# Value rows of product-key experts: from half on VectorE, half on TensorE, to all on TensorE in 64x64 quarters

## The chip, the cores and the metric

The kernel runs on one core of one Trainium2 chip. The metric is the device time of one execution in microseconds (us). All data are fp32.

## What is computed

Two decoder layers over 256 tokens of width 1024, each followed by a product-key expert layer (PEER) with a table of 16384 rows. Layer 0 mixes by sparse attention and retention, layer 1 by a convolution module. The change is in the expert layer, cut here to what matters:

```python
def peer_ffn(h, w_q, sub_keys, u, v):
    q = (xf @ w_q).reshape(T, P_HEADS, 2, P_QDIM // 2)
    s1, s2 = ...                       # two sets of 128 scores for each of 8 heads
    v1, i1 = lax.top_k(s1, 16); v2, i2 = lax.top_k(s2, 16)
    sv, ci = lax.top_k(all 256 sums of v1 and v2, 16)
    eidx = ...                         # 8 heads x 16 picks = 128 rows of the table for each token
    gate = softmax(sv)
    hb = einsum('td,tkd->tk', xb, u[ib])
    act = gelu(hb) * gb
    return einsum('tk,tkd->td', act, v[ib])
```

Each token thus takes 128 picks per layer. A pick is a row of `u` (1024 numbers, for the dot product) and a row of `v` (1024 numbers, for the weighted sum).

## The kernel before, in words

The tokens form two tiles of 128, one token per partition. There are four expert phases `p` = 0 to 3: layer 0 tile 0, layer 0 tile 1, layer 1 tile 0, layer 1 tile 1. A phase has 8 rounds of 16 picks, and a round 4 batches of 4 picks (`RING = 16`, `BATCH = 4`).

The table holds `u` and `v` side by side, 8 KB a row. POOL issues one indirect DMA per pick (`gathers`, L414) that brings one row for each of the 128 tokens, 1 MB, into one of 16 slots of `ring`. It runs at most five gathers ahead of the last one landed (`AHEAD = 5`), and before it fills a slot again it waits for both users of the slot: `v_added` (VectorE) and `v_multiplied` (TensorE). At the start of each round it waits for the slot 0 of the round before, and copies 16 indices (L397).

VectorE (`expert_round`) takes a dot product of each landed slot with the token row (L892, into `hb`). After each batch ScalarE applies Gelu (L562), multiplies with the gate (L566, `act_v`) and writes a 128x128 diagonal matrix with the four weights (L573, `diag`). The weighted sum is split by columns. The first 512 columns are added on VectorE, straight into the residual `x_tok` (L900), four picks behind the dot products. The other 512 are multiplied on TensorE, which accumulates `diag` times the slot in one PSUM bank, `acc` (L1284). `open_sum` puts the residual into `acc` by a product with the identity (L1277), and `close_sum` copies it back (L915):

```python
                pe.matmul(acc, ident[:, :], x_tok[:, p % 2, HALF:D], start=True, stop=False)
...
                    pe.matmul(acc, diag[:, r % (2 * BATCH), :], ring[:, r, D + HALF:2 * D],
                              start=False, stop=(last and r == RING - 1)) \
                        .then_inc(v_multiplied, 1)
...
                dve.tensor_copy(x_tok[:, p % 2, HALF:D], acc).then_inc(x_ready, 1)
```

The order on each engine is written out by hand, and other work is put between the rounds and batches. Beside the rounds of phase 0, and the last four of phases 1 and 2, the product-key heads of the next picks are computed: TensorE makes queries and scores between batches (`heads_in_steps`, L1042, L1263), with a weight chunk of 1 MB for each head, and VectorE picks the best after each round (`heads`). Such rounds are called heads rounds here. Beside the first four rounds of phases 1 and 2 runs the convolution module of the other tile (`conv_beside` on TensorE and ScalarE; `conv_pair` L943, `conv_centre`, `conv_norm`, `conv_out` on VectorE). The last phase has nothing beside it.

Weights come in chunks of 1 MB through SyncE's queue into two buffers (`load_chunks`); a chunk is asked for when the product that used its buffer is done. On the chip all transfers share the same DMA engines.

An fp32 product shows as two weight loads and two matmul records in the trace.

## Time and profile before

| what | value |
|---|---|
| median of 3 runs | 1746.88 us (1746.08 to 1751.19) |
| profiled execution, its span | 1750.9 us (it has no separate time; the span is taken for it) |
| VectorE busy | 1428.1 us, 82% |
| TensorE busy, matmul | 1002.7 us, 57% |
| TensorE weight loads busy | 610.9 us, 35% |
| ScalarE busy | 498.4 us, 28% |
| POOL busy | 775.9 us, 44% |
| moved by DMA | 625.78 MB, mean 357 GB/s |

The rows further down are of four kinds. A group of instructions has its count, its busy time, the mean of one in ns, and the idle time of the engine before it with what ended it. A window gives the busy time of each engine in a stretch, the granted TensorE clock (1.00 is 2.4 GHz, 0.50 is 1.2 GHz), the DMA share (mean busy share of the core's 16 DMA engines; over 1 when packets overlap) and the rate. A timeline merges neighbouring instructions of one kind: start, length, count. Busy shares of the whole span are means over stages that have different limits.

### The profile page before, as it was taken

The page shows a single profiled execution, that of the slowest core. Times are in us where ns is not written, and L with a number is a line of the kernel's source. Part 1 is how long each engine was busy: PE and PEld are TensorE (multiplying, and loading weights), DVE is VectorE, ACT ScalarE, POOL GpSimd, SP SyncE. Part 2 cuts the span into 40 slices and gives each one's busy share as a digit, 9 for nine tenths or more (in the row PEclk, how much of TensorE's full clock was granted, in tenths as well). Part 3 has the DMA queues.
Part 4 walks back from the last instruction along what each step waited for, and adds up shares of the span by engine and source line. Part 5 has one row for each costly group of instructions (what it writes and reads, how often), then busy time and mean ns, then how long its engine had stood idle before and what let it go on. Part 6 is the DMA issues. An engine that isn't in the chain of part 4 may idle for free.

```text
span 1750.9 us, 17116 instructions
## 1 busy us (share of the span) xinstructions
PE 1002.7 (57%) x3934; PEld 610.9 (35%) x3934; DVE 1428.1 (82%) x3330; ACT 498.4 (28%) x1442; POOL 775.9 (44%) x565
## 2 busy tenths in 40 slices
PE   7998663555443653465455555355644456555655
PEld 7785442333331331333333333133422332222222
DVE  2755594999999889894999999988599999877776
ACT  2222220333222522232223242223222233222222
POOL 0003431434434578852344448874333345544551
PEclk9999777787777886676777777678777777776777
DMA  9147989799999999898999998899899998999996
GB/s 356 55 133 301 410 303 366 290 379 385 385 384 402 420 364 368 315 393 318 408 389 378 402 371 338 323 341 418 310 382 395 406 394 335 422 422 422 422 422 266
DMA packets 149994, 625.78 MB, mean 357 GB/s; under 512 B 9648, under 2 KB 76976, under 8 KB 84400
## 3 DMA queue, kind: packets, MB, share of 16 engines
q0 software_dynamic: 73728, 536.90, 75.7%
q1 hardware_dynamic: 76208, 88.20, 14.8%
q8 instruction: 24, 0.39, 0.1%
q14 instruction: 34, 0.28, 0.0%
HBM read 624.02 MB, written 1.05 MB: 357 GB/s over the span
## 4 chain that ended last, share of the span: by engine, by line
DVE 43%; PE 20%; DMA 17%; issue 11%; ACT 4%; DVEq 3%; ACTq 1%; POOL 0%; POOLq 0%
DVE ring L892 15%; DMA ring<-experts_dram,idx_now 11%; DVE x_tok L900 9%; PE pm L1042 9%; PE side L1284 7%; DVE conv_buf L943 7%; DMA wbuf<-w_o_dram 3%; DMA wbuf<-w_dram 3%; ACT act_v L566 1%; PE side L1042 1%; DVE top_i L825 1%; DVE rest L826 1%; DVE top_i L838 1%; ACTq L569 1%; DVE best_i L844 1%
## 5 line engine op out<-in xcount | busy, mean ns | idle before, releaser
L414 POOL DMA_INDIRECT ring<-experts_dram,idx_now x512 | 745.4, 1456 | 633.5 <-DMA ring<-experts_dram,idx_now 247.1
L1284 PE MATMUL side<-ring,diag 128*128 128x512 f32 x1024 | 597.0, 737 | 555.7 <-ACT diag L573 555.6
L892 DVE SCALAR_TENSOR_TENSOR ring<-ring,h_tok 128x1024 f32<-128x1024 f32 x512 | 615.7, 1220 | 55.8 <-DMA ring<-experts_dram,idx_now 50.7
L1284 PEld LDWEIGHTS side<-ring,diag 128*128 128x128 f32 x1024 | 232.6, 239 | 863.9 <-ACT diag L573 625.4
L900 DVE SCALAR_TENSOR_TENSOR x_tok<-ring,act_v,x_tok 128x512 f32<-128x512 f32 x512 | 383.8, 750 | 26.1 <-ACT act_v L566 20.3
L562 ACT ACTIVATE ge<-hb 128x4 f32<-128x4 f32 x128 | 26.3, 205 | 701.3 <-DVE ring L892 701.3
L573 ACT ACTIVATE diag<-ident,act_v 128x128 f32<-128x128 f32 x512 | 163.8, 390 | 15.9 <-issue 2.2
L397 POOL COPY idx_now<-eidx 128x16 uint32 x32 | 24.3, 760 | 258.1 <-DVE x_tok L900 184.3
L943 DVE SCALAR_TENSOR_TENSOR conv_buf<-conv_buf,chan_sb 128x128 f32<-128x128 f32 x480 | 126.7, 347 | 0.0
L1042 PEld LDWEIGHTS side<-h_t,wbuf 128*128 128x128 f32 x1024 | 119.3, 192 | 15.3 <-issue 15.3
L1042 PE MATMUL side<-h_t,wbuf 128*128 128x128 f32 x1024 | 119.5, 275 | 0.0
L566 ACT ACTIVATE act_v<-ge,gates 128x1 f32<-128x1 f32 x512 | 109.0, 283 | 15.6 <-issue 10.9
L1042 PE MATMUL pm<-h_t,wbuf 128*128 128x128 f32 x512 | 63.8, 286 | 21.8 <-DMA wbuf<-w_dram 21.8
L1042 PEld LDWEIGHTS pm<-h_t,wbuf 128*128 128x128 f32 x512 | 63.4, 202 | 30.4 <-DMA wbuf<-w_dram 23.5
L553 ACT ACTIVATE expo<-lead 128x16 f32<-128x16 f32 x32 | 6.6, 208 | 227.6 <-DVE lead L853 227.6
L822 DVE MAX8 top_v<-side 128x8 f32<-128x128 f32 x64 | 15.6, 288 | 63.7 <-PE side L1263 63.7
L562 ACT ACT_TABLE_LOAD x46 | 59.0, 1283 | 3.4 <-issue 2.5
L1042 PE MATMUL pm<-conv_buf,ring 128*128 128x128 f32 x448 | 53.7, 280 | 0.2 <-DVE ring L770 0.2
L1042 PEld LDWEIGHTS pm<-conv_buf,ring 128*128 128x128 f32 x448 | 52.3, 194 | 1.4 <-DVE ring L770 0.6
L1042 PE MATMUL pm<-wbuf,h_t 128*128 128x256 f32 x128 | 33.4, 420 | 27.2 <-DMA wbuf<-w_dram 23.1
L1042 PE MATMUL pm<-wbuf,conv_buf 128*128 128x256 f32 x64 | 22.9, 536 | 42.2 <-DMA wbuf<-w_o_dram 42.2
L1036 PE MATMUL pm<-ident,h_tok 128*128 128x128 f32 x56 | 12.6, 405 | 57.5 <-DVE h_tok L663 57.5
(188 smaller groups left out, 838.0 us busy)
## 6 DMA issues: line engine op xcount, KB each, us to landing
wbuf<-wq_dram SPq DMA_DIRECT2D x32, 1024.0 KB, 25.8
wbuf<-w_dram SPq DMA_DIRECT2D x24, 1024.0 KB, 19.8
ring<-w_in_dram SPq DMA_DIRECT2D x5, 2048.0 KB, 20.0
wbuf<-w_o_dram SPq DMA_DIRECT2D x8, 1024.0 KB, 17.1
ring<-experts_dram,idx_now POOLq DMA_INDIRECT x512, 11.5
gain<-gains_dram SPq DMA_DIRECT2D x7, 512.0 KB, 13.9
ring<-w_in_dram SPq DMA_DIRECT2D x1, 1696.0 KB, 10.1
x_tok<-x_dram SPq DMA_DIRECT2D x2, 512.0 KB, 4.7
```

Of the source, the lines that this page charges most:

```text
L397: pool.tensor_copy(idx_now[:, half, :], eidx[:, t, ds(i * (2 * RING) + half * RING, RING)]) \
L414: pool.indirect_dma_start(ring[:, r, :], None, table[layer], bass.IndirectOffsetOnAxis(idx_now[:, half, r:r + 1], 0)) \
L562: act.activation(ge[:, c], hb[:, c], ACT.Gelu)
L566: last = act.activation(act_v[:, r:r + 1], ge[:, r:r + 1], ACT.Copy, scale=gates[:, t, ds(i * RING + r, 1)])
L569: act.drain()
L573: act.activation(diag[:, (b % 2) * BATCH + j, :], ident[:, :], ACT.Copy, scale=act_v[:, r:r + 1]).then_inc(diag_ready, 1)
L825: dve.max_index(top_i[:, b, j, 0:8], top_v[:, b, j, 0:8], side[b, j])
L892: dve.scalar_tensor_tensor(out=ring[:, r, 0:D], in0=ring[:, r, 0:D], scalar=1.0, in1=h_tok[:, t, :], op0=ALU.mult, op1=ALU.mult, accum_out ...
L900: dve.scalar_tensor_tensor(out=xs, in0=ring[:, r, D:D + HALF], scalar=act_v[:, r:r + 1], in1=xs, op0=ALU.mult, op1=ALU.add).then_inc(v_add ...
L943: step = dve.scalar_tensor_tensor(out=dst, in0=src, scalar=tap, in1=dst, op0=ALU.mult, op1=ALU.add)
L1042: last = pe.matmul(dst, lhs(k), rhs(k), start=(k == 0), stop=(k == KD - 1))
L1284: pe.matmul(acc, diag[:, r % (2 * BATCH), :], ring[:, r, D + HALF:2 * D], start=False, stop=(last and r == RING - 1)) \
```

## The change

The weighted sum moves wholly to TensorE. Two picks are taken together, and each of their products is cut into quarters: 64 rows (tokens) by 64 columns of the array. For tokens 0 to 63, the even pick goes to PSUM partitions 0 to 63 and the odd one to 64 to 127; for tokens 64 to 127 the reverse. With two row halves, two halves of the 1024 columns (`c`) and two picks a pair has eight products of 64x64 by 512. The sums stand in four PSUM banks, `acc[half][c]`, and each bank holds two partial sums, of even and of odd picks, which `close_sum` adds across partitions. The diagonals are 64 wide. The candidates of the heads (`cand`) leave PSUM for SBUF, and the products of the convolution and of the attention output share two banks of `pm` where they had four.

```diff
-HALF = D // 2
+HALF = P // 2
+COLS = D // 2
...
-        diag = sb("diag", [P, 2 * BATCH, P])
+        diag_all = sb("diag_all", [P, 8 * P])
+        diag = diag_all[:, 0:2 * BATCH * HALF].rearrange("p (k c) -> p k c", k=2 * BATCH)
+        cand = diag_all[:, 4 * P:8 * P].rearrange("p (h a b) -> p h a b", h=2, a=P_TOP)
+        ident2 = sb("ident2", [P, HALF])
...
-        acc = side[:, 2, :]
-        cand = side[:, 3, :].rearrange("p (h a b) -> p h a b", h=2, a=P_TOP)
+        acc = [[side[:, 2, :], side[:, 3, :]], [pm[:, 1024:1536], pm[:, 1536:2048]]]
...
-                            pool.wait_ge(v_added, i * (2 * RING) + freed)
                             pool.wait_ge(v_multiplied, i * (2 * RING) + freed)
...
-                        act.activation(diag[:, (b % 2) * BATCH + j, :], ident[:, :], ACT.Copy,
+                        act.activation(diag[:, (b % 2) * BATCH + j, :], ident2[:, :], ACT.Copy,
                                        scale=act_v[:, r:r + 1]).then_inc(diag_ready, 1)
...
-                def add_v(r):
-                    n = p * PICKS + r
-                    if r % BATCH == 0:
-                        dve.wait_ge(act_ready, i * RING + (n + BATCH))
-                    dve.wait_ge(v_added, i * RING + (n + RING))
-                    dve.scalar_tensor_tensor(out=xs, in0=ring[:, r, D:D + HALF], scalar=act_v[:, r:r + 1], in1=xs,
-                                             op0=ALU.mult, op1=ALU.add).then_inc(v_added, 1)
...
             def close_sum(p):
 
+                t = p % 2
                 dve.wait_ge(v_multiplied, RING + (p + 1) * PICKS)
-                dve.tensor_copy(x_tok[:, p % 2, HALF:D], acc).then_inc(x_ready, 1)
+                for i in range(2):
+                    rows = slice(i * HALF, (i + 1) * HALF)
+                    for c in range(2):
+                        dve.tensor_copy(x_tok[rows, t, c * COLS:(c + 1) * COLS], acc[i][c][rows, :])
+                dve.drain()
+                for i in range(2):
+                    rows, others = slice(i * HALF, (i + 1) * HALF), slice((1 - i) * HALF, (2 - i) * HALF)
+                    for c in range(2):
+                        xs = x_tok[rows, t, c * COLS:(c + 1) * COLS]
+                        last = dve.tensor_tensor(xs, xs, acc[i][c][others, :], ALU.add)
+                last.then_inc(x_ready, 1)
...
-                for r in range(RING):
-                    n = p * PICKS + r
-                    pe.wait_ge(diag_ready, i * RING + (n + 1))
-                    pe.matmul(acc, diag[:, r % (2 * BATCH), :], ring[:, r, D + HALF:2 * D],
-                              start=False, stop=(last and r == RING - 1)) \
-                        .then_inc(v_multiplied, 1)
...
+                for r0 in range(0, RING, 2):
+                    n = p * PICKS + r0
+                    pe.wait_ge(diag_ready, i * RING + (n + 2))
+                    pe.sem_inc(pair_on, 1)
+                    for c in range(2):
+                        for r in (r0, r0 + 1):
+                            for half in range(2):
+                                rows = slice(half * HALF, (half + 1) * HALF)
+                                j = (half + r) % 2
+                                step = pe.matmul(acc[half][c][j * HALF:(j + 1) * HALF, :], diag[rows, r % (2 * BATCH), :],
+                                                 ring[rows, r, D + c * COLS:D + (c + 1) * COLS],
+                                                 start=False, stop=(last and r >= RING - 2))
+                            if c:
+                                step.then_inc(v_multiplied, 1)
```

Two more edits follow from the banks. `open_sum` has eight quarter products for one. The first two additions of the attention output of tile 1 (`add_projected`) stand one round earlier, and TensorE waits for them before it uses their bank again; in the convolution, a product waits for the glu of the tile two before it, not four.

On TensorE, the first batches of phase 0. Before, four full products stood between two queries (in these rows `side` and `pm` are PSUM, `diag` the diagonals, `ring` the slots, `wbuf` a weight chunk):

```order
L1284 MATMUL side<-ring,diag 128x512 x4
L1042 MATMUL side<-h_t,wbuf 128x128 x16
L1284 MATMUL side<-ring,diag 128x512 x4
L1042 MATMUL side<-h_t,wbuf 128x128 x16
L1284 MATMUL side<-ring,diag 128x512 x4
L1263 MATMUL side<-keys_sb,q_t 128x128 x2
```

Now the last pair of picks of the third batch, up to the scores, reads:

```order
L1298 MATMUL side<-ring,diag_all 64x512
L1298 MATMUL pm<-ring,diag_all 64x512
L1298 MATMUL side<-ring,diag_all 64x512
L1298 MATMUL pm<-ring,diag_all 64x512
L1298 MATMUL side<-ring,diag_all 64x512
L1298 MATMUL pm<-ring,diag_all 64x512
L1298 MATMUL side<-ring,diag_all 64x512
L1298 MATMUL pm<-ring,diag_all 64x512
L1265 MATMUL side<-keys_sb,q_t 128x128 x2
L1042 MATMUL pm<-wbuf,conv_buf 128x256 x8
```

Each row of four products with 128x512 (one batch) has become two pairs of eight with 64x512, alternating between the banks of the two token halves.

On VectorE, the end of phase 0 before:

```order
L892 SCALAR_TENSOR_TENSOR ring,hb<-ring,h_tok 128x1024
L900 SCALAR_TENSOR_TENSOR x_tok<-ring,act_v,x_tok 128x512
L892 SCALAR_TENSOR_TENSOR ring,hb<-ring,h_tok 128x1024
L900 SCALAR_TENSOR_TENSOR x_tok<-ring,act_v,x_tok 128x512 x5
L915 COPY x_tok<-side 128x512
L659 RECIPROCAL rstd<-root 128x1
L663 SCALAR_TENSOR_TENSOR h_tok<-x_tok,rstd,gain 128x1024
L924 MEMSET conv_buf 128x8x30
L892 SCALAR_TENSOR_TENSOR ring,hb<-ring,h_tok 128x1024 x5
```

And now:

```order
L897 SCALAR_TENSOR_TENSOR ring,hb<-ring,h_tok 128x1024 x16
L907 COPY x_tok<-side 64x512 x2
L907 COPY x_tok<-pm 64x512 x2
L913 TENSOR_TENSOR x_tok<-x_tok,side 64x512 x2
L913 TENSOR_TENSOR x_tok<-x_tok,pm 64x512 x2
L664 RECIPROCAL rstd<-root 128x1
L668 SCALAR_TENSOR_TENSOR h_tok<-x_tok,rstd,gain 128x1024
L923 MEMSET conv_buf 128x8x30
```

The 16 dot products of the round stand in one row with nothing between them, and closing the sum is eight instructions of 64 partitions.

On POOL, from the tenth slot of a round to the start of the next, with the semaphores waited for. Before:

```order
L414 DMA ring<-experts_dram,idx_now 128x2048 [waits gathered9,v_added,v_multiplied]
L414 DMA ring<-experts_dram,idx_now 128x2048 [waits gathered10,v_added,v_multiplied]
L394 REGISTER_ALU
L395 REGISTER_ALU [waits picks_ready]
L397 ISA [waits v_added]
L397 COPY idx_now<-eidx 128x16
L414 DMA ring<-experts_dram,idx_now 128x2048 [waits gathered11,v_multiplied,idx_copied,v_added]
```

And now:

```order
L418 DMA ring<-experts_dram,idx_now 128x2048 [waits v_multiplied,gathered9]
L418 DMA ring<-experts_dram,idx_now 128x2048 [waits v_multiplied,gathered10]
L399 REGISTER_ALU
L400 REGISTER_ALU [waits picks_ready]
L402 ISA [waits v_multiplied]
L402 COPY idx_now<-eidx 128x16
L418 DMA ring<-experts_dram,idx_now 128x2048 [waits gathered11,idx_copied,v_multiplied]
```

The waits for VectorE's additions are gone, and the copy of the next indices, too, waits for TensorE.

## Rows read from the trace of the kernel before

**Rows 1.** The page, 40 equal slices of the span: busy tenths, DMA tenths, GB/s

```profile
DVE  2755594999999889894999999988599999877776
...
DMA  9147989799999999898999998899899998999996
GB/s 356 55 133 301 410 303 366 290 379 385 385 384 402 420 364 368 315 393 318 408 389 378 402 371 338 323 341 418 310 382 395 406 394 335 422 422 422 422 422 266
```

**Rows 2.** Windows: us, busy PE, PEld, DVE, ACT, POOL, TensorE clock, DMA share, GB/s

```profile
405.00:453.60 48.60, 25.22 (x104) 15.36 (x104) 44.76 (x116) 13.16 (x44) 19.51 (x17) 0.75 0.98 388
...
587.10:819.50 232.40, 126.75 (x488) 79.71 (x488) 195.62 (x468) 73.51 (x181) 148.28 (x71) 0.75 0.93 364
...
1015.40:1246.80 231.40, 124.91 (x488) 79.72 (x487) 195.74 (x468) 73.49 (x181) 146.73 (x68) 0.77 0.90 352
...
1503.10:1701.70 198.60, 112.77 (x158) 43.08 (x157) 152.31 (x242) 53.11 (x185) 98.48 (x85) 0.75 1.01 422
```

**Rows 3.** Windows: full traffic, a dip, and the two stretches of the sum

```profile
374.00:412.00 38.00, 13.29 (x60) 8.41 (x59) 34.10 (x99) 10.11 (x34) 12.18 (x13) 0.76 1.02 411
...
803.00:809.00 6.00, 6.00 (x19) 4.39 (x18) 0.42 (x1) 0.00 (x0) 0.00 (x0) 0.70 0.39 128
...
318.00:1472.70 1154.70, 614.49 (x2416) 375.11 (x2415) 1029.61 (x2534) 348.03 (x1014) 580.21 (x383) 0.76 0.95 373
1472.70:1735.70 263.00, 155.51 (x219) 59.23 (x217) 207.36 (x330) 70.73 (x249) 128.69 (x108) 0.75 1.00 418
```

**Rows 4.** Timeline of VectorE in a heads round: start us, us

```profile
406.15 1.22 DVE L892 SCALAR_TENSOR_TENSOR ring<-ring,h_tok 128x1024 f32<-128x1024 f32 x1
...
407.30 1.22 DVE L892 SCALAR_TENSOR_TENSOR ring<-ring,h_tok 128x1024 f32<-128x1024 f32 x1
...
427.88 1.22 DVE L892 SCALAR_TENSOR_TENSOR ring<-ring,h_tok 128x1024 f32<-128x1024 f32 x1
...
429.69 1.23 DVE L892 SCALAR_TENSOR_TENSOR ring<-ring,h_tok 128x1024 f32<-128x1024 f32 x1
```

**Rows 5.** The page, groups by line, and a DMA issue with its us to landing

```profile
L414 POOL DMA_INDIRECT ring<-experts_dram,idx_now x512 | 745.4, 1456 | 633.5 <-DMA ring<-experts_dram,idx_now 247.1
L1284 PE MATMUL side<-ring,diag 128*128 128x512 f32 x1024 | 597.0, 737 | 555.7 <-ACT diag L573 555.6
...
L900 DVE SCALAR_TENSOR_TENSOR x_tok<-ring,act_v,x_tok 128x512 f32<-128x512 f32 x512 | 383.8, 750 | 26.1 <-ACT act_v L566 20.3
...
L943 DVE SCALAR_TENSOR_TENSOR conv_buf<-conv_buf,chan_sb 128x128 f32<-128x128 f32 x480 | 126.7, 347 | 0.0
...
L915 DVE COPY x_tok<-side 128x512 f32<-128x512 f32 x4 | 2.8, 692 | 6.0 <-PE side L1284 6.0
...
ring<-experts_dram,idx_now POOLq DMA_INDIRECT x512, 11.5
```

**Rows 6.** Timeline of TensorE (last row: chain of waits): start us, us, records

```profile
42.60 1.15 PE L1105 MATMUL side<-ring 32*128 32x256 f32 x16
...
89.08 1.09 PE L1193 MATMUL side<-ring 128*64 128x128 f32 x16
...
102.25 7.07 PE L1042 MATMUL side<-wbuf,conv_buf 128*128 128x256 f32 x32
...
248.51 3.73 PE L1042 MATMUL side<-h_t,wbuf 128*128 128x128 f32 x32
...
432.77 3.70 PE side L1284 x8
```

**Rows 7.** Waits in 307 to 550 us: total us, times, longest

```profile
POOL idx_now L397 <- DVE x_tok L900: 57.3, 5, 22.0
...
POOL ring L414 <- PE side L1284: 25.1, 18, 2.0
```

**Rows 8.** The chain of waits, 754 to 822 us: start us, us

```profile
777.36 24.32 DMA wbuf<-w_dram
```

**Rows 9.** The page, an instruction queue: packets, MB, share

```profile
q8 instruction: 24, 0.39, 0.1%
```

More of the change, by code:

```diff
@@ L258, in hybrid_decoder_trunk_kernel @@
         a_at = [side_flat[:, 1536:2048], pm[:, 1536:2048]]
-        wo_at = [[side_flat[:, c * 512:c * 512 + WCOLS] for c in range(4)], [pm[:, c * 512:c * 512 + WCOLS] for c in range(4)]]
+        wo_at = [[side_flat[:, c * 512:c * 512 + WCOLS] for c in range(4)], [pm[:, c % 2 * 512:c % 2 * 512 + WCOLS] for c in range(4)]]
         def norm_at(e):
@@ L887, in expert_round @@
                 rounds = PICKS // RING
-                xs = x_tok[:, t, 0:HALF]
-                def dot(r):
+                for r in range(RING):
+                    if between:
+                        between(r)
                     dve.wait_ge(gathered[r], i * 16 + 16 * (p * rounds + 1))
@@ L991, in _ @@
             heads(0, 1)
+            for c in range(2):
+                add_projected(1, c)
             expert_round(0, 1)
             heads(0, 2)
-            for c in range(4):
+            for c in range(2, 4):
                 add_projected(1, c)
@@ L1204, in output_product @@
                 pe.wait_ge(b_t_ready, t + 1)
+                if t and c >= 2:
+                    pe.wait_ge(projected_added, 4 + c - 1)
                 w = chunk(W_O[t] + c + (t and c // 2 * 2))
@@ L1276, in open_sum @@
                     pe.wait_ge(x_ready, (0, 3, 5, 7)[p])
-                pe.matmul(acc, ident[:, :], x_tok[:, p % 2, HALF:D], start=True, stop=False)
-            def expert_round(p, i, between=None, last=False):
-                for r in range(RING):
-                    n = p * PICKS + r
-                    pe.wait_ge(diag_ready, i * RING + (n + 1))
-                    pe.matmul(acc, diag[:, r % (2 * BATCH), :], ring[:, r, D + HALF:2 * D],
-                              start=False, stop=(last and r == RING - 1)) \
-                        .then_inc(v_multiplied, 1)
-                    if between and (r + 1) % BATCH == 0:
-                        between(r // BATCH)
+                for c in range(2):
+                    for j in range(2):
+                        for i in range(2):
+                            rows = slice(i * HALF, (i + 1) * HALF)
+                            out_rows = slice(j * HALF, (j + 1) * HALF)
+                            pe.matmul(acc[i][c][out_rows, :], ident[rows, out_rows], x_tok[rows, p % 2, c * COLS:(c + 1) * COLS],
+                                      start=True, stop=False)
+            def expert_round(p, i, between=None, last=False):
+                for r0 in range(0, RING, 2):
+                    n = p * PICKS + r0
+                    pe.wait_ge(diag_ready, i * RING + (n + 2))
+                    pe.sem_inc(pair_on, 1)
+                    for c in range(2):
+                        for r in (r0, r0 + 1):
[7 more added lines that the diff above has]
+                                step.then_inc(v_multiplied, 1)
+                    if between and (r0 + 2) % BATCH == 0:
+                        between(r0 // BATCH)
             def conv_in(t, c):
@@ L1294, in conv_in @@
                 for j in range(2):
-                    last = product(pm[:, (c % 4) * 512 + j * P:(c % 4) * 512 + (j + 1) * P],
+                    last = product(pm[:, c % 2 * 512 + j * P:c % 2 * 512 + (j + 1) * P],
                                    lambda k: w[:, k, j * P:(j + 1) * P], lambda k: h_t[:, k, :])
```

36 lines of the change are left out of this document (15 added, 21 removed).

## The prediction, made before the changed kernel ran

> **What bounds the kernel now.** I read the page's slices first [rows 1]. VectorE is mostly at 8 or 9 tenths from the eighth slice to the thirty-fourth, and that invites the conclusion that VectorE is the bound. The transfer rows beneath say more: the DMA engines are at 8 or 9 tenths in the same slices, and the rate only settles at 422 GB/s in the last stage.
>
> So the stages have to be read one by one. By the windows [rows 2], the last stage (1503 to 1702 us, five of the eight rounds of the last token tile) has DMA share 1.01 and 422 GB/s: it is bound by transfers, and nothing VectorE does less can shorten it. A round with product-key heads (405.0 to 453.6 us, 48.6 us for 16 picks and two weight chunks of 1 MB) has VectorE busy 44.8 us, yet the DMA share is already 0.98 at 388 GB/s. The convolution stages (587.1 to 819.5 and 1015.4 to 1246.8 us) have 0.93 and 0.90 at 364 and 352 GB/s. Where the transfers lose time is seen by cutting finer [rows 3]: undisturbed traffic of picks with weights beside it (374 to 412 us) runs at share 1.02 and 411 GB/s, while a dip such as 803 to 809 us has 0.39. The waits of POOL, which issues the gathers, name the cause [rows 7]: in 307 to 550 us it stood 57.3 us before the copy of the next 16 indices, waiting for a ring slot that VectorE's addition frees. The kernel is thus bound by transfers that VectorE interrupts. VectorE's time is worth only the gaps that it tears into them.
>
> **The change part by part.** *Taken from VectorE:* 512 additions at L900, 750 ns of one and 383.8 us together [rows 5]. Start to start, two dot products without an addition between them are 1.15 us apart and with one 1.81 us [rows 4]; 16 dot products then take 18.4 us instead of 29. A heads round on VectorE falls from 48.6 to about 18.4 + 22.7 = 41.1 us, where 22.7 us is what lies between the end of dot product 16 (430.9 us) and the next first one (453.6 us). That is below what its transfers need, so they become the bound.
>
> *Put on TensorE:* the other 512 columns. Each pick had one 128x512 product, two matmul records; warm, eight records take 3.70 us [rows 6], so 0.93 us per pick with start-up and 0.86 without. Now a pair of picks has eight 64-row, 64-column products over 512 columns. If the four quarters run together, two groups of two records each take 4 x 0.43 = 1.7 us per pair, 0.86 per pick: no more than now. Whether they do decides the case. The trace shows both halves of it. Two column halves (L1193, 128*64) do 16 records of 128 columns in 1.09 us, though 32 records on the full array take 3.73 us, 0.117 each. Four row groups (L1105, 32*128) do 16 records of 256 columns in 1.15 us, where the full array takes 7.07 us for 32, 0.22 each [rows 6]. So rows together and columns together each overlap nearly ideally; both at once appears nowhere. I take 0.86 us warm (about 1.7 at the half clock), and between there and four times that lie the rivals.
>
> The Trainium skill, "TensorE: Matmul & The Clock Gate", Part 3, gives measured gains of packing below the ideal, 3.07 times for four row tiles and 6.32 for nine in both directions; by 3.07 an estimate for a pick would be 1.1 us warm, which would still lie under the transfers and leave the sum as it is. The trace agrees for rows alone: 16 x 0.22 = 3.5 us against 1.15 is 3.1 times.
>
> *ScalarE:* the diagonals halve in width. I cost that at nothing: the chain of Gelu, gate and four diagonals remains. *POOL:* each gather waits on one semaphore less, but slots come back in pairs and only from TensorE, so slot 0 is free, and the index copy can start, up to one pair later (3.4 us at the half clock). The granted clock averages 0.75 there [rows 2], a mix of the two levels. Nearly hidden: five gathers are in flight, at 2.5 us each (198.6 us / 80 in the last stage) or 2.9 beside weights (45.9 / 16, below).
>
> *Closing a tile's sum:* one copy of 0.69 us [rows 5] becomes four copies, a drain and four additions over 64 partitions and the same 512 columns. The number of partitions has no row; by the columns it is 8 x 0.69 = 5.5 us, 4.8 more, between half of it (if 64 partitions were cheaper) and 6 with the drain. Four times: the last is on the path to the output and counts in full; the other three lie in breaks in which gathers go on. Opening a sum is 8 products for one, under 1 us more, hidden by the Gelu chain of the first batch. The candidates move from PSUM to SBUF, the convolution's products share two banks instead of four and are reused after two; the glu they wait for comes from a step that VectorE has by then passed, so nothing. Two additions of the attention output move one round earlier, 0.4 us each, nothing.
>
> *The sum.* Up to 318 us: no change. VectorE waits there for products behind weight chunks, which the edit leaves. From 318 to 1472.7 us, 1154.7 us at share 0.95 and 373 GB/s [rows 3]. Filled without gaps, by the share it would be 1154.7 x 0.95 / 1.02 = 1075 us, by the bytes 1154.7 x 373 / 411 = 1048 us: a gain of 80 or 107, and I take the middle, 93, since the weights' small packets cost share that the bytes don't show. Not all gaps close. Two convolution stages still end behind a weight chunk that takes 24.3 us to land [rows 8] while TensorE, and with it four ring slots, stands; two tiles close with about 29 us before the next dot product (5.6 waiting for the last products, from 430.9 to 436.5 us in the heads round, 5.5 closing, 17 heads, which is the rest of the 22.7, and one norm of about a dot product), against eleven gathers of 2.5 to 2.9 us that can still be issued. I leave 5 us for each of these four and 5 for the twelve heads rounds: 25 us. Gain 93 - 25 = 68. From 1472.7 to 1735.7 us: share 1.00, gain 0. Tail: 4.8 us more. Together 63 us less: the profiled execution's 1750.9 us become 1688, and the median of the runs, 1746.9 us, which lies 4 us below it, becomes **1684 us**.
>
> **The rivals.** *A, the forecast:* four quarters together, transfers filled. Own range 1645 (all 107, no gap left) to 1717 us (80, with the gaps taken at 45). Chance 0.60.
>
> *B, latency keeps the gaps:* the dips in the convolution stages and tile breaks are made by the wait for weight chunks and by long VectorE blocks that remain. Then only the twelve heads rounds gain, from 48.6 to 45.9 us (48.6 x 388 / 411), 32 us, less 4.8: 27 us, 1720 us. For it: the 24.3 us wait. Against: the dips also follow the blocks of 15.8 us of convolution (126.7 us / 8) [rows 5], during which the ring would now be less behind. Chance 0.18.
>
> *C, only two quarters at once:* 1.71 us per pick warm. A heads round has 16 x 1.71 + 8 us of other products, 35 of 46 us, so TensorE isn't the bound, but every slot comes back later and I would leave 60 us of gaps instead of 25: 1719 us. Chance 0.08.
>
> *D, one quarter at a time:* this ends slower. 3.43 us per pick, 55 + 8 = 63 us for a heads round against 48.6 (13 rounds, with the one before 356 us; 187 us), 55 against 39.8 in the last tile (8 rounds, 121 us), and 39 more in each convolution stage (126.7 us busy now, 64 x 2.26 us more, against 232): about 2130 us. It decides from 2.4 us per pick on, (46 - 8) / 16. Against it are both overlaps in [rows 6]. Chance 0.08.
>
> *E, TensorE's loop is fetched anew in each pass:* a heads loop grows from 16 + 36 to 64 + 36 products, each four instructions, 208 to 400. One instruction queue moved 24 packets of together 0.39 MB [rows 9], 16 KB each, so the loop now spans more of them. If each pass had to fetch behind the gathers, with their 11.5 us to landing as the upper bound (the lower is nothing), slot 0 would come 11.5 us late in ten loop rounds: with 12 us idle in each, 1684 + 120 = 1804 us. Chance 0.06. The Trainium skill, "Runtime: NRT & Kernel Launch", Instruction fetch mechanics, says that a taken branch out of the present window forces such a fetch, and also that TensorE's instruction memory holds 2048 instructions, by which 400 would fit; no row here shows its size.
>
> **How the numbers follow.** The time is A's. A measurement of this kernel can tell 0.3% (5 us) from no change. A gives 0.58 faster and the rest to same and slower, B and C 0.20 faster, 0.05 same and 0.01 slower, D and E 0.14 slower: faster 0.78, same 0.06, slower 0.16. The range leaves out D and E and reaches over B and C: 1650 to 1730 us.
>
> **What would show it.** Right: quarter products starting some ns apart in fours, under 2 us per pair warm; dot products 1.15 us apart after each block; heads rounds of 45 to 47 us with share 1.01 or 1.02; convolution stages of 205 to 215 us; the last tile's rounds unchanged at 39.8 us; about 5 us more after the last product. Wrong: a pair of 3.4 us or more at the full clock (C, D), pauses of TensorE at each loop start (E), heads rounds faster but convolution stages still near 230 us (B), or heads rounds still at 48 us though VectorE stands idle in them.

## The result, and the profile of the changed kernel

The changed kernel takes 1771.25 us (median of 4 runs, 1766.83 to 1773.54); the kernel before, on the same chip, takes 1749.04 us (4 runs, 1746.08 to 1752.86). The ratio is 1.0116, with a 95% interval of 1.0092 to 1.0140: the change makes the kernel slower by 1.2%, where 3.6% faster was forecast. The profiled execution has a span of 1771.2 us against 1750.9 us.

The page first. Rows answer to [rows 1] and [rows 5]:

```profile
PE 1029.6 (58%) x7062; PEld 570.4 (32%) x7062; DVE 1098.6 (62%) x2846; ACT 468.2 (26%) x1442; POOL 746.3 (42%) x566
...
DVE  2655274666668877734766687691477766544454
...
GB/s 354 52 131 313 413 262 376 327 374 381 386 401 396 414 335 349 371 413 266 388 405 390 395 295 355 357 368 412 263 388 385 386 370 339 421 422 422 422 422 216
...
L1298 PE MATMUL side<-ring,diag_all 64*64 64x512 f32 x2048 | 585.6, 721 | 496.6 <-ACT diag_all L577 496.5
...
L826 DVE MAX8 top_v<-side 128x8 f32<-128x128 f32 x64 | 15.7, 290 | 211.3 <-PE side L1265 211.2
L974 DVE TENSOR_TENSOR x_tok<-x_tok,pm 128x256 f32<-128x256 f32 x8 | 3.0, 418 | 84.6 <-PE pm L1042 84.5
```

VectorE was relieved just as the diff says: it is busy in 62% of the span, and the slices that stood at 8 or 9 tenths stand mostly at 6 to 8. TensorE's products cost nothing extra (585.6 us where they had 597.0 [rows 5]; those into `pm`, 585.5 us, run beside those into `side`). Yet the mean rate of the transfers is 353 GB/s where it was 357, and the two slices just behind the convolution stages have fallen to 266 and 263 GB/s, from 318 and 310 [rows 1]. The last two rows of groups show where VectorE's freed time went: it is waited away, 211.2 us at the first operation of the heads and 84.5 us at the residual addition of the convolution.

The same in windows. Columns as in [rows 2]: us, busy PE, PEld, DVE, ACT, POOL, TensorE clock, DMA share, GB/s. In order: a heads round, the first and the second convolution stage, a round of the last tile, and 803 to 809 us.

```profile
403.30:451.90 48.60, 25.27 (x200) 13.46 (x200) 33.71 (x100) 12.10 (x44) 18.87 (x17) 0.75 0.97 384
...
582.20:819.80 237.60, 127.33 (x872) 76.22 (x872) 152.88 (x405) 70.04 (x181) 147.15 (x74) 0.77 0.95 376
...
1021.50:1254.00 232.50, 132.84 (x872) 78.14 (x871) 152.06 (x404) 70.10 (x181) 138.57 (x68) 0.76 0.91 356
...
1593.30:1633.10 39.80, 23.60 (x128) 7.56 (x128) 19.75 (x33) 9.76 (x37) 20.51 (x17) 0.71 1.01 422
...
803.00:809.00 6.00, 0.56 (x2) 0.50 (x2) 0.00 (x0) 0.00 (x0) 0.18 (x1) 0.50 1.02 411
```

A heads round lasts 48.60 us, to the tenth what it lasted before [rows 2], with 11 us less of VectorE in it. The first convolution stage is 5.2 us longer, with 43 us less of VectorE in it. And the dip at 803 to 809 us (0.39, 128 GB/s in [rows 3]) is gone: the transfers now run straight through it, and the stage is longer all the same. Measured from the first dot product of each round to the next, the whole adds up:

| stretch (us) | before | after | difference |
|---|---|---|---|
| start to round 3 | 356.3 | 353.7 | -2.6 |
| four heads rounds | 194.3 | 194.2 | -0.1 |
| last round of that tile (no heads) | 36.5 | 34.3 | -2.2 |
| first convolution stage | 232.4 | 237.6 | +5.2 |
| next four heads rounds (the one that closes a tile: 50.3, 55.4) | 195.9 | 201.7 | +5.8 |
| second convolution stage | 231.4 | 232.5 | +1.1 |
| next four heads rounds (the closing one: 50.1, 54.7) | 195.6 | 200.4 | +4.8 |
| last tile, to its last dot product | 294.6 | 296.6 | +2.0 |
| after the last dot product | 13.9 | 20.2 | +6.3 |

Inside the convolution stages the relief did pay at first: their first three rounds together take 156.9 and 154.1 us where they took 167.7 and 166.4. Their last rounds took it back, 80.6 and 78.4 us where they had 64.7 and 65.0.

So there are two questions: why twelve rounds of heads gained nothing, and what makes 20 us at the end of the convolution stages and where tiles close. The chain of waits answers the first, over one heads round (start us, us, what):

```profile
403.27 4.68 DVE ring L897 x8
...
410.07 1.08 PE side L1298
...
415.74 3.77 PE side L1042 x32
...
423.10 3.77 PE side L1042 x32
...
430.46 0.64 PE side L1265 x4
...
434.70 0.66 PE side L1265 x4
...
451.94 1.23 DVE ring L897
```

Four dot products (4.7 us), then Gelu and diagonals (2.1 us), and from 410.07 to 435.4 us TensorE without a pause: four batches of products (L1298), two queries of 3.77 us (L1042), and the scores of the two heads (L1265), the second of which stands in its queue **behind the last batch**. Only then can VectorE finish the heads, in 16.5 us, and start the next round. 4.7 + 2.1 + 25.3 + 16.5 = 48.6 us: this ring goes through TensorE, and it is as long as the whole round was before. In windows (columns as above), TensorE's piece and its first batch alone:

```profile
410.07:435.40 25.33, 25.27 (x200) 13.44 (x200) 12.12 (x24) 8.53 (x32) 11.54 (x11) 0.92 0.92 358
...
410.07:415.74 5.67, 5.67 (x33) 1.80 (x33) 5.67 (x11) 2.46 (x11) 0.91 (x2) 0.64 0.87 355
```

TensorE is busy in 25.27 of the 25.33 us. Behind 23.4 us of idleness its first batch is granted a mean clock of 0.64 and takes 5.7 us, where the later batches, at 1.00, take 3.6; that, too, is part of the ring.

The kernel before had the same ring already. In its round of 405.0 to 453.6 us TensorE worked from 411.52 to 436.9 us with one pause, of 0.17 us, before its last batch of products, and VectorE then stood 1.25 us for the scores behind that batch:

```profile
432.77 3.70 PE L1284 MATMUL side<-ring,diag 128*128 128x512 f32 x8 [0.17 <-ACT diag L573]
...
437.07 0.50 DVE L822 MAX8 top_v<-side 128x8 f32<-128x128 f32 x2 [1.25 <-PE side L1263]
```

In the changed kernel VectorE's timeline shows the wait (the last number in brackets is idle us before the operation, and what ended it):

```profile
421.61 0.08 DVE L897 DVE_READ_ACCUMULATOR ring<-ring,h_tok 128x1 f32 x1
431.25 0.50 DVE L826 MAX8 top_v<-side 128x8 f32<-128x128 f32 x2 [9.56 <-PE side L1265]
435.49 0.50 DVE L826 MAX8 top_v<-side 128x8 f32<-128x128 f32 x2 [3.74 <-PE side L1265]
```

For the first convolution stage, the chain of waits at its end, to be set beside the 24.32 us of [rows 8], and the transfers from 755 to 815 us by queue (packets, MB, share):

```profile
767.44 3.67 PE pm L1042 x16
...
771.12 37.18 DMA wbuf<-w_dram
...
808.44 6.21 PE pm L1042 x16
```

```profile
q0 software_dynamic: 2981, 21.68, 87.4%
q1 hardware_dynamic: 2883, 2.92, 14.5%
```

The fourth and last chunk of the second convolution weight needs 37.18 us to land. Between 755 and 815 us the gathers' queue (q0) moves 2981 packets and the weights' queue (q1) 2883, almost one for one; but a packet of a gather is a row of 8 KB, and one of a weight chunk a row of 1 KB, so weights get 49 of 410 GB/s. At that rate 1 MB takes 21 us by itself. The rest of the 37 us is the third chunk, asked for at 760.8 us and landed at about 787.3 us (TensorE starts on it at 787.4), with the fourth, asked for at 771.1 us, behind it.

The 24.32 us of [rows 8] belong to the third chunk, and it was not spared the crowd: while it was on its way in the kernel before, the two queues moved

```profile
q0 software_dynamic: 1189, 8.68, 86.7%
q1 hardware_dynamic: 1272, 1.29, 15.6%
```

again one for one. What differed was the fourth chunk. It was asked for at 790.7 us, and at 790.55 us POOL had issued its last gather for a while, since TensorE freed no slot:

```profile
809.50 0.93 POOL L414 DMA_INDIRECT ring<-experts_dram,idx_now  x1 [17.82 <-PE side L1284]
```

Once the gathers in flight had landed, the weights had the wires almost to themselves (794 of their packets against 55 from 802 to 808 us), and the fourth chunk landed in 16.9 us. The dip at 803 to 809 us was thus what let it through. From the request for the third chunk to the end of the stage it is 42.1 us before and 59.0 us after; the third chunk is asked for 11.7 us earlier in the stage now, and 16.9 - 11.7 makes the 5.2 us. The Trainium skill, "DMA: Bandwidth & Descriptors", Queues, rings and completion order, has each DMA engine go round its queues packet by packet; the trace agrees, with one packet for one as the profile counts them (2981 against 2883, and 1189 against 1272).

### The profile page after: what moved, and what is told of

Same layout as the page of the kernel before. It is cut to its first block, busy times and chain, and to the rows that moved or that the text cites. A ratio compares the mean times of both kernels' runs of the same rounds, so it can differ in the third digit from the quotient of the medians.

```text
span 1771.2 us, 22155 instructions
## 1 busy us (share of the span) xinstructions
PE 1029.6 (58%) x7062; PEld 570.4 (32%) x7062; DVE 1098.6 (62%) x2846; ACT 468.2 (26%) x1442; POOL 746.3 (42%) x566
## 4 chain that ended last, share of the span: by engine, by line
PE 36%; DMA 29%; DVE 25%; ACT 3%; issue 3%; DVEq 3%; ACTq 1%; POOL 0%; POOLq 0%
DMA ring<-experts_dram,idx_now 21%; PE side L1298 17%; PE pm L1042 9%; DVE ring L897 8%; PE side L1042 7%; DVE conv_buf L942 5%; DMA wbuf<-w_dram 4%; DMA wbuf<-w_o_dram 4%; PE side L1265 1%; DVE top_i L829 1%; ACT diag_all L577 1%; DVE rest L830 1%; ACT act_v L570 1%; DVE top_i L842 1%; PE pm L1298 1%
## 5 line engine op out<-in xcount | busy, mean ns | idle before, releaser
L418 POOL DMA_INDIRECT ring<-experts_dram,idx_now x512 | 718.5, 1403 | 635.1 <-issue 375.3
L1298 PE MATMUL side<-ring,diag_all 64*64 64x512 f32 x2048 | 585.6, 721 | 496.6 <-ACT diag_all L577 496.5
L897 DVE SCALAR_TENSOR_TENSOR ring<-ring,h_tok 128x1024 f32<-128x1024 f32 x512 | 599.8, 1224 | 171.0 <-DMA ring<-experts_dram,idx_now 165.8
L1298 PE MATMUL pm<-ring,diag_all 64*64 64x512 f32 x2048 | 585.5, 721 | 0.0
L1298 PEld LDWEIGHTS side<-ring,diag_all 64*64 64x64 f32 x2048 | 180.2, 162 | 835.5 <-issue 828.7
L1298 PEld LDWEIGHTS pm<-ring,diag_all 64*64 64x64 f32 x2048 | 165.8, 161 | 0.0
L826 DVE MAX8 top_v<-side 128x8 f32<-128x128 f32 x64 | 15.7, 290 | 211.3 <-PE side L1265 211.2
L577 ACT ACTIVATE diag_all<-ident,act_v 128x64 f32<-128x64 f32 x512 | 136.3, 336 | 17.3 <-issue 4.1
L1042 PEld LDWEIGHTS side<-h_t,wbuf 128*128 128x128 f32 x1024 | 116.8, 192 | 25.7 <-issue 25.7
L1042 PE MATMUL side<-h_t,wbuf 128*128 128x128 f32 x1024 | 122.6, 278 | 0.0
L1042 PE MATMUL pm<-h_t,wbuf 128*128 128x128 f32 x512 | 69.4, 300 | 26.5 <-DMA wbuf<-w_dram 26.5
L1042 PEld LDWEIGHTS pm<-h_t,wbuf 128*128 128x128 f32 x512 | 66.4, 213 | 40.4 <-DMA wbuf<-w_dram 30.0
L1042 PE MATMUL pm<-wbuf,h_t 128*128 128x256 f32 x128 | 38.8, 470 | 54.6 <-DMA wbuf<-w_dram 53.1
L974 DVE TENSOR_TENSOR x_tok<-x_tok,pm 128x256 f32<-128x256 f32 x8 | 3.0, 418 | 84.6 <-PE pm L1042 84.5
L1042 PE MATMUL pm<-conv_buf,ring 128*128 128x128 f32 x448 | 53.7, 280 | 0.2 <-DVE ring L774 0.2
L1042 PEld LDWEIGHTS pm<-conv_buf,ring 128*128 128x128 f32 x448 | 52.3, 194 | 1.4 <-DVE ring L774 0.6
## 6 DMA issues: line engine op xcount, KB each, us to landing
wbuf<-w_o_dram SPq DMA_DIRECT2D x8, 1024.0 KB, 21.7
ring<-experts_dram,idx_now POOLq DMA_INDIRECT x512, 11.7
```

Source lines behind the costliest of these rows:

```text
L418: pool.indirect_dma_start(ring[:, r, :], None, table[layer], bass.IndirectOffsetOnAxis(idx_now[:, half, r:r + 1], 0)) \
L577: act.activation(diag[:, (b % 2) * BATCH + j, :], ident2[:, :], ACT.Copy, scale=act_v[:, r:r + 1]).then_inc(diag_ready, 1)
L897: dve.scalar_tensor_tensor(out=ring[:, r, 0:D], in0=ring[:, r, 0:D], scalar=1.0, in1=h_tok[:, t, :], op0=ALU.mult, op1=ALU.mult, accum_out ...
L1042: last = pe.matmul(dst, lhs(k), rhs(k), start=(k == 0), stop=(k == KD - 1))
L1298: step = pe.matmul(acc[half][c][j * HALF:(j + 1) * HALF, :], diag[rows, r % (2 * BATCH), :], ring[rows, r, D + c * COLS:D + (c + 1) * COLS ...
```

## The experiments

The theory after this reading, **theory 1**: the heads rounds are held by the ring through TensorE, whose length is set by the scores standing behind the last batch, and the convolution stages by weight chunks that share the wires packet by packet. Its rivals: what holds the round is the amount of work on TensorE whatever its order, or the slots of the ring that come back in pairs, or the transfers of the round themselves.

**The scores ahead of the last batch.** TensorE's order in a heads round, alone (in all heads rounds but the first two of the kernel; indentation cut):

```diff
- between(r0 // BATCH)
+ b = r0 // BATCH
+ if not early or b < 2:
      between(b)
+ elif b == 2:
+     between(2)
+     between(3)
```

> Changed kernel, but TensorE makes the second head's scores before the last batch of picks and not after it. Theory 1 (a ring of waits: first batch of dot products, Gelu and diagonals, TensorE's whole round with both heads' products, then VectorE's heads, closes at 48.3 us): the heads can start 3.4 to 4.4 us sooner, heads rounds fall from 48.3 to 44.5 to 46 us, twelve of them give 30 to 45 us, median near 1733. Theory 2 (the transfers of a heads round, at share 0.97, are themselves the limit): rounds stay within 0.7 us of 48.3, median 1765 to 1771.

Measured: 1733.02 us (6 runs, 1721.53 to 1738.75), ratio 0.9901 to the kernel before (0.9865 to 0.9937). The heads rounds take 44.0 to 44.7 us; one of them in a window, and VectorE's timeline in it:

```profile
395.00:439.40 44.40, 24.56 (x200) 13.26 (x200) 33.81 (x101) 12.10 (x44) 19.99 (x17) 0.77 1.02 413
```

```profile
422.46 0.94 DVE L826 MAX8 top_v<-side 128x8 f32<-128x128 f32 x4 [7.76 <-PE side L1265]
```

Both heads' scores are there at 422.5 us, one wait instead of two, and the round runs at share 1.02 and 413 GB/s, the traffic that the prediction had asked for. The same instructions, on the same engines, in another order, are 38 us faster. The convolution stages' ends (rounds of 86.8 and 77.8 us) and the closings (55.3 and 54.7 us) do not get better, as theory 1 has it. Of VectorE's work, of the slots in pairs and of the amount of work on TensorE nothing was touched, and the round is 4.2 us shorter. That puts the transfers and the bare amount of work out as the bound of the 48.6 us; what the pairs cost by themselves no run shows.

**The same order in the kernel before.** The edit above, in the old loop.

> The kernel before with the same edit alone. There the four last additions (3.1 us) already cover most of the wait for the last batch, so theory 1 expects the heads 1.5 to 2.5 us sooner, heads rounds of about 46.5 us instead of 48.6, 18 to 30 us in all (median 1720 to 1732). Theory 2: nothing, 1747 to 1750.

Measured: 1737.13 us, ratio 0.9930 (0.9908 to 0.9953). The heads rounds fall from 48.6 to 47.3 us. The direction is right and the size too large: 1.3 us per round, and a median 5 us above the range. VectorE's own ring, with its additions, is just behind the one through TensorE: its last addition of the round ended at 435.4 us in the kernel before, 1.5 us ahead of the last scores. This is what two rings of nearly equal length mean in numbers: the reorder alone brings 1.3 us, the change alone nothing, both together 4.2 us.

**Half of the products.** The loop over the two column halves takes only the first; half of the weighted sum is left out, so this is not a version but a measure of TensorE's share.

```diff
-                     for c in range(2):
+                     for c in range(1):
...
-                             if c:
-                                 step.then_inc(v_multiplied, 1)
+                             step.then_inc(v_multiplied, 1)
```

> Changed kernel; the products of the second half of the 1024 columns are left out, so that half of the weighted sum is missing. TensorE's part of a round shrinks by 16 x 0.43 = 6.9 us and more at the half clock. Theory 1: heads rounds become bound by transfers, 45 to 46.5 us instead of 48.3, and slots come back sooner; median 1720 to 1740. Theory 2: heads rounds stay at 48, only the tail and the convolution rounds gain, median 1755 to 1770.

Measured: 1709.87 us (2 runs), ratio 0.9779 (0.9730 to 0.9828), 10 us below the range expected. Two heads rounds in one window:

```profile
382.90:473.20 90.30, 38.47 (x272) 23.68 (x272) 68.06 (x200) 24.30 (x88) 38.97 (x34) 0.73 1.02 412
```

45 us for a round at share 1.02 (single ones take 42 to 49 us): less work in the ring through TensorE lets the transfers fill, as less waiting does. The scores stand where they stood. So it is the length of the ring that counts, of which the place of the scores is one cause and the products another. Fewer products also give the slots back sooner, so this run alone does not speak against the rival of the slots; the reorder, which leaves them in pairs, shows that the pairs do not keep the round at 48.6 us.

**Closing without the additions.** The drain and the four additions of the closing are removed; one half of each pair's sum is left out.

```diff
-                 dve.drain()
-                 for i in range(2):
...
-                         last = dve.tensor_tensor(xs, xs, acc[i][c][others, :], ALU.add)
```

> Changed kernel; closing a sum only copies, so that of every two picks one is missing from the result. Closing falls from 5.2 to 2.6 us, four times. If all four closings lie on the path: 10 us less, median 1761. If only the last does: 2.6 us, 1769.

Measured: 1765.46 us (4 runs, 1760.59 to 1767.14), ratio 1.0100 (1.0064 to 1.0136). That is 6 us below the changed kernel by the medians, between the two expectations, but the intervals of the two ratios overlap, so the total alone does not show a gain. The traces do: the closing rounds take 52.6 and 52.4 us instead of 55.4 and 54.7, and the part after the last dot product 16.4 us instead of 20.2, of which 2.6 us are the additions and 1.2 a shorter wait for the last products. At the first of the four closings nothing is seen (the two rounds around it take 75.7 and 75.6 us).

**The second convolution weight in long rows.** Only this weight is laid out by chunks in HBM, so that a chunk of 1 MB is 128 rows of 8 KB instead of 1024 of 1 KB.

```diff
-                     sp.dma_start(wbuf[:, n % WBUF, :, :], view[:, :, c * WCOLS:(c + 1) * WCOLS]) \
+                     if len(view.shape) == 2:
+                         dst, src = wbuf[:, n % WBUF, :, :].rearrange("p k c -> p (k c)"), view[c * P:(c + 1) * P, :]
...
+                     sp.dma_start(dst, src) \
...
+def by_chunk(w):
+
+    return w.reshape(KD, P, -1, WCOLS).transpose(2, 1, 0, 3).reshape(-1, KD * WCOLS)
```

> Changed kernel; only the convolution's second weight matrix is laid out so that a 1 MB chunk is 128 rows of 8 KB, as a gather is, where it was 1024 rows of 1 KB. Theory 3 (the chunk lands late because the DMA engines share by packet, 360 GB/s of gathers against 50 of weights): these chunks land in 5 to 10 us instead of 25 and 35, the last round of each convolution stage falls from 80.6 and 78.4 us to 52 to 62, median 1731 to 1750. Theory 4 (the block at the end of the stage is made by TensorE's order and VectorE's steps): landing times change, but the rounds by less than 8 us each, median above 1758.

Measured: 1745.68 us (10 runs, 1738.98 to 1756.48, the slowest being the profiled one), ratio 0.9966 (0.9949 to 0.9984). The chain of waits over the same place:

```profile
780.73 9.04 DMA wbuf<-w_dram
...
795.25 37.72 DMA wbuf<-wq_dram
```

The chunk that took 37.18 us takes 9.04, and the stages' last rounds fall from 80.6 and 78.4 to 53.0 and 53.2 us. But the rounds behind them grow from 48.6 and 48.3 to 63.8 and 65.5 us. A chunk of query weights, still in rows of 1 KB, now stands in the chain there with 37.72 us, but it can't be all that makes these rounds long, as the next experiment shows. Of the 52.8 us by which the last rounds got shorter, 32.4 came back in the rounds behind them.

**All weights in long rows**, in the changed kernel, and **the same in the kernel before**:

> Changed kernel with all 64 weight chunks in rows of 8 KB. Theory 3: also the first two rounds (70 and 66 us, behind chunks of the output projection) fall to about 50 us each, the heads rounds stay near 48 us because they are bound by TensorE's round and the heads behind it; median 1685 to 1710.

> The kernel before with all weight chunks in rows of 8 KB. Heads rounds stay at 48.6 us (VectorE), the first two fall from 70 to 50 to 55 us, the convolution stages lose the waits for chunks but stay bound by VectorE at 210 to 220 us; median 1685 to 1705. The change would then still be worth nothing by itself.

Measured: 1705.59 us (4 runs, ratio 0.9744, 0.9709 to 0.9779) and 1693.50 us (4 runs, ratio 0.9682, 0.9652 to 0.9712). With short weight rows the change costs 22 us, with long ones 12. So some 10 of its 22 us are the late chunks. The rounds behind the convolution stages stay long in the changed kernel, 63 and 59 us, with no short row left. The first of them in a window:

```profile
754.10:817.40 63.30, 31.36 (x208) 16.57 (x208) 34.57 (x102) 14.48 (x46) 24.62 (x23) 0.72 1.01 421
```

The transfers fill it without a gap: 22 gathers land in it, six more than a round uses, since the stage before it ended with its gathers still to come. So the last round of a stage and the round behind it must be read together: the first such pair takes 129.3 us in the changed kernel and 113.2 us with long rows, 113.3 us in the kernel before and 103.9 us with long rows. The other heads rounds stay at 48.0 to 49.5 us in the changed kernel and at 48.3 to 48.8 in the one before, and the closings stay (54.9 and 54.2 against 50.2 and 50.0). The closings and the tail cover the 12 us: they are 4.7, 4.2 and 5.0 us longer than in the kernel before with long rows.

The convolution stages of the kernel before were 232.4 and 231.4 us [rows 2]. With long rows they are, a little above the 210 to 220 us expected:

```profile
549.30:771.70 222.40, 123.53 (x488) 77.52 (x488) 195.70 (x469) 73.52 (x181) 143.93 (x71) 0.76 0.91 374
967.50:1186.90 219.40, 121.15 (x488) 76.36 (x487) 195.60 (x467) 73.50 (x181) 144.78 (x68) 0.78 0.89 360
```

**Both edits together**, in the changed kernel, and in the kernel before:

> Changed kernel with early scores and all weights in rows of 8 KB: both causes taken away. Heads rounds near 44 to 45 us (18 transfers of 1 MB at 422 GB/s are 44.7 us), first rounds 50 us, convolution stages 200 to 210 us: median 1640 to 1665, below both kernels.

> The kernel before (half of the sum on VectorE) with early scores and all weights in rows of 8 KB: the same two edits as in the fastest run, without the change. Theory 1 has VectorE as the bound of a heads round here, 47.3 us as with early scores alone, so the median is 1675 to 1685, and the change is worth 12 to 22 us once the two other limits are gone. Rival (the change is worth nothing even then, all the gain is the two edits): 1658 to 1668.

Measured: 1662.69 us (4 runs, 1653.84 to 1671.06), ratio 0.9502 (0.9450 to 0.9553), and 1684.11 us (3 runs, 1678.66 to 1691.56), ratio 0.9601 (0.9565 to 0.9637). Each median is within its expected range. Windows of the changed kernel with both edits, a heads round and the two convolution stages:

```profile
365.80:410.80 45.00, 25.18 (x200) 13.38 (x200) 33.68 (x101) 12.10 (x44) 19.73 (x17) 0.77 1.01 418
535.50:749.30 213.80, 127.75 (x872) 71.89 (x872) 152.73 (x405) 70.04 (x181) 142.58 (x69) 0.78 0.91 373
944.30:1148.10 203.80, 123.32 (x872) 70.42 (x871) 151.95 (x403) 70.11 (x181) 136.37 (x63) 0.79 0.90 364
```

The change itself is worth 1684.1 - 1662.7 = 21 us by the medians and 1.0% (17 us) by the ratios, once what it waits for is out of the way. These two kernels ran on different chips, each beside the kernel before; the intervals do not overlap. By the traces most of it lies in the convolution stages, which take 224.2 and 222.5 us in the kernel before with both edits. The very same move of additions to TensorE costs 22 us in one surrounding and gains about 20 in another.

**The heads ahead of the closing.** In the fastest version so far, the last half of the heads goes ahead of the closing of the tile on VectorE.

```diff
                  expert_round(p, 7)
-                 close_sum(p)
                  heads(p + 1, 3)
+                 close_sum(p)
```

> Changed kernel with early scores and long rows, and VectorE computes the last heads of phases 1 and 2 before it closes the sum, so that the wait for the last products (6.7 us) lies under the heads. The rounds that close a tile fall from 55.8 and 54.7 to about 51 us if VectorE's block is what counts; 3 to 8 us in all, median 1655 to 1660. If the transfers refill the loss anyway: no difference from 1663.

Measured: 1657.77 us (4 runs, 1653.32 to 1661.27), ratio 0.9461 (0.9429 to 0.9492). The closing rounds fall by 1.3 and 1.0 us only, to 54.5 and 53.7 us, not to the 51 us expected. Its chain of waits shows why:

```profile
937.55 1.29 DVE x_tok L917 x2
...
938.86 1.06 ACT h_tok L439
...
940.06 1.28 ACT L441
...
941.36 0.30 ACT root L441
```

The eight instructions of the closing no longer wait for the last products, but ScalarE's part of the norm (square, table load and root, 1.06 + 1.28 + 0.30 us), which before lay beneath the heads, now stands open behind them. One exposed stretch was exchanged for another. It is the fastest version measured and beats both kernels of the case, by 92 us the one before; whether it beats the previous one can't be told (5 us, overlapping intervals).

## Why the prediction was wrong, point by point

**The bound.** "The kernel is thus bound by transfers that VectorE interrupts." The first half holds for the last tile (39.8 us a round before and after), and the second was only one of two causes. The wait that the prediction read from [rows 7], POOL for VectorE's addition, is real, 57.3 us; what it hid is that a ring of the same length through TensorE stood directly behind it, with only 0.17 us of pause in it. Over the whole run of the changed kernel the waits (total us, times, longest) read:

```profile
POOL idx_now L402 <- PE pm L1298: 226.6, 17, 27.7
DVE top_v L826 <- PE side L1265: 211.2, 28, 23.3
...
DVE x_tok L974 <- PE pm L1042: 84.5, 3, 41.9
```

Before, the first was 184.3 us (19 times, for VectorE), the second and the third 63.7 us (15 times) and 41.6 us (4 times, 14.4 at most). POOL stands before the same copy of indices as in [rows 7], with the releaser changed from VectorE to TensorE.

**The step that failed: "A heads round on VectorE falls from 48.6 to about 18.4 + 22.7 = 41.1 us ... That is below what its transfers need, so they become the bound."** The 18.4 us was right (the dot products are 1.15 us apart, the last one ends at 421.6 us). The 22.7 us was not a constant. It is 5.6 us of waiting for the last products and 17 us of heads, as the prediction itself splits it. The 17 us held (16.5). The 5.6 us were counted from the last dot product, as if the products came at a fixed distance behind it; but it is the end of TensorE's piece that sets them, and that hangs on the first batch of the round and not on the last dot product. The last scores leave TensorE at 435.4 us whatever VectorE does; with the last dot product done at 421.7 us the wait became 13.7 us, the block after the dot products 30.2 us (421.7 to 451.9), and 18.4 + 30.2 = 48.6. The prediction had TensorE's busy time (25.2 us of 48.6 [rows 2]) and compared only such totals with the round ("35 of 46 us, so TensorE isn't the bound", in rival C). Half idle was right; but its 25 us lie in one piece, in the middle of a ring whose other parts, 4.7 + 2.1 + 16.5 us, cannot lie beside them. The reorder and the halved products show it from two sides. The prediction's own last sign, "heads rounds still at 48 us though VectorE stands idle in them", is what came.

**The gaps of the convolution stages** (5 us for each taken off the gain). The prediction named the chunk of 24.3 us and took the wait as a constant too. Of the pair of chunks at a stage's end it is the other one that changed: 16.9 us before, in part with no gather beside it, and 37.2 us with the gathers flowing. The gap that the prediction counted as lost traffic was the time in which that chunk got through. Rival B had the stages stay near 230 us; they became 237.6 and 232.5, so even B was too friendly here. The runs with long rows show that the landing of chunks is worth 10 us of the change's loss, and 56 us to the kernel before on its own. Of those 56, some 36 are in the first two rounds (69.2 and 70.2 us, now 50.8 and 52.2), which the prediction left alone, and 21 at the ends of the two stages.

**The closings** (4.8 us, "the last ... counts in full; the other three lie in breaks in which gathers go on"). The price per closing was about right: 5.2 us for the eight instructions, 1.3 per pair, where the sum had 5.5. Timeline of VectorE at the end:

```profile
1759.80 1.28 DVE L907 COPY x_tok<-side 64x512 f32<-64x512 f32 x2 [8.75 <-PE pm L1298]
1761.09 1.30 DVE L907 COPY x_tok<-pm 64x512 f32<-64x512 f32 x2
1762.47 1.30 DVE L913 TENSOR_TENSOR x_tok<-x_tok,side 64x512 f32<-64x512 f32 x2
1763.78 1.28 DVE L913 TENSOR_TENSOR x_tok<-x_tok,pm 64x512 f32<-64x512 f32 x2
```

The tail grew by 6.3 us, 4.6 from this and most of the rest from the last batch of products (6.6 us where it had 5.2). Two of the other three closings are on the path as well, 4.6 to 5.1 us each; the removal of the additions took 2.8 and 2.3 us from them. With the heads rounds bound by a ring, a longer block on VectorE has no gathers to hide under.

**What was right.** The four quarters run at once (rival C and D are out), as the timeline of TensorE in the last tile shows:

```profile
1604.08 0.61 PE L1298 MATMUL side<-ring,diag_all 64*64 64x512 f32 x1 [4.09 <-ACT diag_all L577]
1604.09 0.64 PE L1298 MATMUL pm<-ring,diag_all 64*64 64x512 f32 x1
1604.10 0.64 PE L1298 MATMUL side<-ring,diag_all 64*64 64x512 f32 x1
1604.10 0.64 PE L1298 MATMUL pm<-ring,diag_all 64*64 64x512 f32 x1
1604.53 0.59 PE L1298 MATMUL side<-ring,diag_all 64*64 64x512 f32 x1
```

Four records start within 0.02 us, the next four 0.45 us after the first: four such steps are 1.7 us for a pair, as reckoned from the row halves and column halves of [rows 6]. Rival E is out: the instruction queue that moved 24 packets moves 38 in the whole run, and none from the second to the fourth pass of the first heads loop (403.3 to 547.9 us), though each pass should have fetched. The rounds of the last tile stayed at 39.8 us from the third on. The transfers' price of a heads round without gaps, 45.9 us in rival B, was reached (44.4 us), but only by versions with less waiting or less work in the ring.

**What stays open.** The last round of the first convolution stage grew further, to 86.8 us, once the scores went early. No run was made for it. By the trace the chunks are not the cause: from the request for the third chunk on it is 58.8 us, where the change alone has 59.0. The growth lies before it, 27.9 us for 21.7, at share 1.01 in both, with VectorE waiting for gathers that the shorter rounds ahead had left to come. How much the return of slots in pairs costs stays open as well. The chance of 0.16 for slower stood almost wholly on rivals D and E (0.14), both mechanisms that are not there; the ring through TensorE was in no rival. The right side of the range was missed by 41 us.

## What to carry to other kernels

Before taking work from the busiest engine, follow one round as a ring through every engine, once starting from each of them: a queue that serves in order is a constant of that ring, and 25 us in one piece on an engine busy half the time is enough to bound it. Put what another engine waits for ahead of what nobody waits for (38 us here, with no instruction changed), and do it before moving the work. A time to landing, or a gap after a block, read from one trace is not a constant: it holds for what was in flight beside it and for the event that it hangs on. When the gathers no longer stopped, a chunk in short rows beside them landed later (37.2 us for 16.9), and rows as long as the other queue's were the remedy (56 us in the kernel before, 66 in the changed one). And a round that got shorter may have handed its transfers to the next one, so read the two together.

## What the runs showed of the hardware that was not expected

- 64x64 quarters with rows and columns both split overlap nearly ideally here, in spite of the 3.1 times of the four row groups [rows 6]: four products of 512 columns start 0.43 to 0.45 us after the four before them, where eight records of 512 columns on the full array take 3.70 us, 0.46 each [rows 6].
- An operation of VectorE over 64 partitions costs what it costs over 128: 0.65 us for a copy of 512 columns from PSUM (two in 1.28 to 1.30 us), where 128 partitions take 0.69 us [rows 5]. One copy split into two halves of the partitions thus takes 1.28 to 1.30 us for 0.69.
- Two queues share the wires by packets, not by bytes: 2981 packets of 8 KB rows against 2883 of 1 KB rows in 60 us. The last 1 MB of a stage landed in 37.2 us in rows of 1 KB, behind another such chunk, and in 9.0 us in rows of 8 KB.
